# Spreads by transposes, fewer exponent instructions, a conv tap on ScalarE and bias rows spread in DRAM, in an SSM stage

## The reference

```
zxbcdt = rms_norm(x, ln_g) @ in_w          # 40 tiles of 128 columns, and dt
xbc = silu(causal_dwconv(xbc, conv_w, conv_b))        # 4 taps
a_cs = cumsum(a, axis=-1)                  # per head, chunks of 128 tokens
decay_in = exp(segsum(a))                  # exp(a_cs[l] - a_cs[s]), l >= s
y_diag = einsum('bclgn,bcsgn->bcgls', cc, bc) * decay_in @ xc
states = einsum(bc, exp(a_cs[..., -1:] - a_cs), xc)
y_off  = einsum(cc, states_in, exp(a_cs))
...
bias = rel_bias[t5_bucket(dist)]           # attention, 8 heads
```

## Time and profile before

| | |
|---|---|
| median of 3 runs | 2348.98 us (2348.26 to 2349.67) |
| profiled execution | 2351.74 us |
| its span | 2349.9 us |
| PE busy in the span | 2226.8 us, 95% |
| DVE busy | 1483.0 us, 63% |
| ACT busy | 914.2 us, 39% |
| granted TensorE clock, mean | 0.965 |

### The profile page before, as it was taken

The page is one execution under the profiler, slowest core; times in us unless marked ns, Lnnn a source line. Parts: engine busy times, 40 slices in busy tenths (PEclk is TensorE's granted clock), DMA queues, the critical chain, the costliest instruction groups (busy, mean ns, idle before and its releaser), DMA issues.

```text
span 2349.9 us, 26916 instructions
## 1 busy us (share of the span) xinstructions
PE 2226.8 (95%) x10370; PEld 1686.4 (72%) x10370; DVE 1483.0 (63%) x2262; ACT 914.2 (39%) x1379; POOL 0.2 (0%) x4
## 2 busy tenths in 40 slices
PE   8998989999999998999799999998999999899997
PEld 6787775548888886777588888886666667677545
DVE  6588887647777336777677776455566746455334
ACT  4344443114444223777434443233354422343302
POOL 0000000000000000000000000000000000000000
PEclk9998999999999998999799999998999999899999
DMA  4321111123232333111023222332122123111122
GB/s 143 108 65 53 55 63 45 45 81 94 94 98 87 94 101 103 54 55 55 21 96 98 95 94 88 93 110 72 54 70 68 60 72 135 37 46 48 43 83 79
DMA packets 53245, 179.39 MB, mean 76 GB/s; under 512 B 5751, under 2 KB 5879, under 8 KB 52888
## 3 DMA queue, kind: packets, MB, share of 16 engines
q1 hardware_dynamic: 50112, 167.79, 22.7%
q10 hardware_dynamic: 3032, 10.28, 1.2%
HBM read 173.33 MB, written 4.72 MB: 76 GB/s over the span
## 4 chain that ended last, share of the span: by engine, by line
PE 43%; DVE 7%; ACT 2%; issue 1%; DMA 0%; DVEq 0%; ACTq 0%
PE bankpair L271 11%; PE bankpair L272 11%; PE bankpair L275 11%; PE bankpair L279 4%; DVE conv_rows L352 1%; PE bankpair L1200 1%; PE bankpair L1233 1%; PE bankpair L1214 1%; DVE weights_low L306 1%; DVE reciprocals L1473 1%; PE bankpair L1066 1%; DVE padded_rows L1424 1%; ACT L1304 0%; PE bankpair L1075 0%; PE bankpair L1182 0%
## 5 line engine op out<-in xcount | busy, mean ns | idle before, releaser
L271 PE MATMUL bankpair<-scaled_in_high,weights_high 128*128 128x512 f32 x1792 | 731.0, 408 | 12.9 <-DVE padded_rows L1939 4.3
L272 PE MATMUL bankpair<-scaled_in_low,weights_high 128*128 128x512 f32 x1792 | 709.2, 396 | 0.0
L275 PE MATMUL bankpair<-scaled_in_high,weights_low 128*128 128x512 f32 x1792 | 447.9, 389 | 0.0
L295 ACT ACTIVATE weights_high<-weight_ring 128x1024 fp32r<-128x1024 f32 (+2 forms) x304 | 302.5, 995 | 348.1 <-DMA weight_ring<-down_dram 155.8
L271 PEld LDWEIGHTS bankpair<-scaled_in_high,weights_high 128*128 128x128 f32 x1792 | 344.1, 192 | 96.9 <-issue 13.1
L272 PEld LDWEIGHTS bankpair<-scaled_in_low,weights_high 128*128 128x128 f32 x1792 | 343.6, 192 | 76.0 <-issue 6.1
L275 PEld LDWEIGHTS bankpair<-scaled_in_high,weights_low 128*128 128x128 f32 x1792 | 336.7, 188 | 70.3
L306 DVE TENSOR_TENSOR weights_low<-weight_ring,weights_high 128x1024 fp32r<-128x1024 f32 (+2 forms) x304 | 347.8, 1154 | 55.2 <-ACT weights_high L295 46.7
L279 PE MATMUL bankpair<-arena,weight_ring 128*128 128x512 f32 x448 | 199.4, 607 | 2.8 <-DVE arena L1975 1.5
L279 PEld LDWEIGHTS bankpair<-arena,weight_ring 128*128 128x128 f32 x448 | 86.9, 195 | 111.2 <-issue 107.4
L271 PE MATMUL bankpair<-gated_high,weights_high 128*128 128x512 f32 x352 | 139.2, 396 | 0.0
(11 more groups left out here) (325 smaller groups left out, 2456.9 us busy)
## 6 DMA issues: line engine op xcount, KB each, us to landing
weight_ring<-up_dram SPq DMA_DIRECT2D x88, 512.0 KB, 3.4
weight_ring<-w_in_dram SPq DMA_DIRECT2D x70, 512.0 KB, 3.4
weight_ring<-in_w_dram SPq DMA_DIRECT2D x40, 512.0 KB, 3.5
weight_ring<-down_dram SPq DMA_DIRECT2D x32, 384.0 KB, 3.1
weight_ring<-kvq_dram SPq DMA_DIRECT2D x24, 512.0 KB, 3.4
weight_ring<-down_dram SPq DMA_DIRECT2D x32, 320.0 KB, 2.8
weight_ring<-out_a_dram SPq DMA_DIRECT2D x8, 512.0 KB, 3.4
weight_ring<-out_b_dram SPq DMA_DIRECT2D x8, 512.0 KB, 3.5
```

The costliest lines, as they stand in the source:

```text
L271: nc.tensor.matmul(bank, WH[:, high_slot, cell], high, start=(k == 0), stop=False)
L272: nc.tensor.matmul(bank, WH[:, high_slot, cell], low, start=False, stop=False)
L275: mm = nc.tensor.matmul(bank, WL[:, slot, cell], high, start=False, stop=(c == last_k))
L295: nc.scalar.activation(WH[:, (PART0[name] + k) % SLOTS, 0:n], RAW[:, b % SLOTS, 0:n], ACT.Copy).then_inc(high_ready, 1)
```

## The change

- The sums of a unit are spread by eight transposes of a repeated column of `CSTK` (tokens on partitions) in place of eight products.
- One minimum on 128x1024, min(spread sums, own sum), takes the place of the eight subtractions with a minimum; the own sum is subtracted by the bias of the exponential, so that ACT runs eight exponentials of 128x128. The last column of the result serves in place of `FX`, so that its copies, its difference and its exponential go. The two exponentials of the spread sums become one.
- DVE's order in a unit: the copy of the last exponentials and the product with C now stand before the wait for ACT, the scaling for the state and the product with C B behind it; the last releases PE's y.
- The first conv tap of the 24 x, B and C rows is an ACT instruction (Identity with scale and bias), ahead of ACT's weight split; DVE waits for it before the other three.
- The bias rows of all eight heads are one pair of products with eight columns behind tile 0, one copy (8x640), one write to DRAM; eight DRAM to DRAM transfers, one behind each of rows 2 to 9 on ACT's queue, spread them over 128 rows. Attention's read waits for them.

```diff
+        BROWS = nc.dram_tensor("bias_rows", (AH, 640), F32, kind="Internal").ap()
...
+        def first_tap(act, b, taps_and_bias, taps):
+            return nc.scalar.activation(CV[:, b, :], U[:, b, 3:3 + T], ACT.Identity, bias=taps_and_bias(taps),
+                                        scale=taps_and_bias(taps - 1))
+        def other_taps(step, done, b, taps_and_bias, taps):
+            for k in range(taps - 1):
+                at = 3 - (taps - 1) + k
+                (done if k == taps - 2 else step).step(nc.vector.scalar_tensor_tensor(
+                    CV[:, b, :], U[:, b, at:at + T], taps_and_bias(k), CV[:, b, :], ALU.mult, ALU.add))
...
+            act.wait_ge(brow_spread, 16 * AH)
             skewed = bass.AP(tensor=DSCR.tensor, offset=P - 1, ap=[[639, P], [P * 640, AH], [1, T]])
@@ PE
             for j in range(GROUP_TILES):
                 in_tile(0, j)
-                if j >= GROUP_TILES - AH:
-                    bias_row(j - (GROUP_TILES - AH))
+                if j == 0:
+                    pe.wait_ge(aux_in, 32)
+                    nc.tensor.matmul(BANK[2][0:AH, :], REL[0:33, :], BUCK[0:33, 0:T], start=True, stop=True)
+                    nc.tensor.matmul(BANK[3][0:AH, 0:P], REL[0:33, :], BUCK[0:33, T:640],
+                                     start=True, stop=True).then_inc(brow_done, 1)
...
                     for h in range(SSM_HG):
-                        nc.tensor.matmul(BANK[2 + h // 4][:, (h % 4) * P:(h % 4 + 1) * P],
-                                         IDENT[0:32, SSM_HG * g + h:SSM_HG * g + h + 1].to_broadcast([32, P]),
-                                         CSR[0:32, tok], start=True, stop=True)
+                        nc.tensor.transpose(BANK[2 + h // 4][:, (h % 4) * P:(h % 4 + 1) * P],
+                                            CSTK[:, c, SSM_HG * g + h:SSM_HG * g + h + 1].to_broadcast([P, P]), IDENT)
@@ ACT
             def rows(g, j):
                 n = GROUP_TILES * g + j
+                if j >= GT:
+                    act.wait_ge(gemm_free, TILE0["in_w"] + n + 1)
+                    first_tap(act, n % 2, ssm_taps(g, j), 4).then_inc(row_tap, 1)
                 split_high(act, BASE["in_w"] + n + 3)
...
                 rows(0, j)
-                b = j - (GROUP_TILES - AH)
-                if b >= 0:
-                    act.wait_ge(brow_done, b + 1)
-                    nc.scalar.activation(BROW[:, b, 0:T], BANK[2][:, :], ACT.Copy).then_inc(brow_ready, 1)
-                    nc.scalar.activation(BROW[:, b, T:640], BANK[3][:, 0:P], ACT.Copy).then_inc(brow_ready, 1)
-            act.wait_ge(brow_ready, 2 * AH)
-            act.dma_start(DSCR.rearrange("h p m -> p h m"), BROW).then_inc(brow_out, 16)
+                if j == 0:
+                    act.wait_ge(brow_done, 1)
+                    nc.scalar.activation(BROW[0:AH, :], BANKPAIR[1][0:AH, :, :].rearrange("p a t -> p (a t)")[:, 0:640],
+                                         ACT.Copy).then_inc(brow_ready, 1)
+                    act.wait_ge(brow_ready, 1)
+                    act.dma_start(BROWS, BROW[0:AH, :]).then_inc(brow_out, 16)
+                if j == 2:
+                    act.wait_ge(brow_out, 16)
+                if j >= GROUP_TILES - AH:
+                    b = j - (GROUP_TILES - AH)
+                    act.dma_start(DSCR[b], BROWS[b:b + 1, :].to_broadcast([P, 640])).then_inc(brow_spread, 16)
...
-                    for q in range(2):
-                        nc.scalar.activation(ECS[:, 4 * q:4 * q + 4, :],
-                                             BANK[2 + q][:, :].rearrange("p (h t) -> p h t", t=P),
-                                             ACT.Exp).then_inc(e_ready, 1)
+                    nc.scalar.activation(ECS, BANKPAIR[1][:, :, :].rearrange("p a (h t) -> p (a h) t", t=P),
+                                         ACT.Exp).then_inc(e_ready, 1)
                     act.wait_ge(d_ready, u + 1)
-                    nc.scalar.activation(DEC, DEC, ACT.Exp).then_inc(d_exp, 1)
-                    nc.scalar.activation(FX, FX, ACT.Exp).then_inc(d_exp, 1)
+                    for h in range(SSM_HG):
+                        at = SSM_HG * g + h
+                        exp = nc.scalar.activation(DEC[:, h, :], DEC[:, h, :], ACT.Exp, bias=NEGCS[:, c, at:at + 1])
+                    exp.then_inc(d_exp, 1)
@@ DVE
                 if j >= GT:
-                    conv(dve, step, cv, n % 2, lambda k: par("ssm_conv", 5 * ((GT + 2) * g + j - GT) + k), 4)
+                    dve.wait_ge(row_tap, (GT + 2) * g + j - GT + 1)
+                    other_taps(step, cv, n % 2, ssm_taps(g, j), 4)
...
             tt.step(nc.vector.tensor_copy(CSTK, b6[:, :, 32:64]))
+            tt.step(nc.vector.tensor_scalar(NEGCS, CSTK, -1.0, None, ALU.mult))
...
-                    for q in range(2):
-                        step.step(nc.vector.tensor_copy(etot[:, 4 * q:4 * q + 4], BANK[2 + q][:, P - 1:T:P]))
-                    step.step(nc.vector.tensor_tensor(fx, etot, CSTK[:, c, heads], ALU.subtract))
-                    for h in range(SSM_HG):
-                        ins = nc.vector.tensor_scalar(dec[:, h, :], BANK[2 + h // 4][:, (h % 4) * P:(h % 4 + 1) * P],
-                                                      CSTK[:, c, SSM_HG * g + h:SSM_HG * g + h + 1], 0.0,
-                                                      ALU.subtract, ALU.min)
-                    dr.step(ins)
-                    dve.wait_ge(d_exp, 2 * u + 2)
-                    step.step(nc.vector.tensor_tensor(dec, dec, CBM.unsqueeze(1).to_broadcast([P, SSM_HG, P]), ALU.mult))
+                    dr.step(nc.vector.tensor_tensor(dec, BANKPAIR[1][:, :, :].rearrange("p a (h t) -> p (a h) t", t=P),
+                                                    CSTK[:, c, heads].unsqueeze(2).to_broadcast([P, SSM_HG, P]), ALU.min))
                     step.step(nc.vector.tensor_copy(etot, ecs[:, :, P - 1]))
-                    mce.step(nc.vector.tensor_tensor(ecs, ecs, xb[:, GT + 1, tok].unsqueeze(1).to_broadcast([P, SSM_HG, P]),
-                                                     ALU.mult))
+                    step.step(nc.vector.tensor_tensor(ecs, ecs, xb[:, GT + 1, tok].unsqueeze(1).to_broadcast([P, SSM_HG, P]),
+                                                      ALU.mult))
+                    dve.wait_ge(d_exp, u + 1)
                     if c < NT - 1:
-                        xf.step(nc.vector.tensor_tensor(x_f, xdt, fx.unsqueeze(2).to_broadcast([P, SSM_HG, 64]), ALU.mult))
+                        xf.step(nc.vector.tensor_tensor(x_f, xdt, dec[:, :, P - 1:P].to_broadcast([P, SSM_HG, 64]), ALU.mult))
+                    mce.step(nc.vector.tensor_tensor(dec, dec, CBM.unsqueeze(1).to_broadcast([P, SSM_HG, P]), ALU.mult))
```

More of the change, by code:

```diff
@@ L175, in three_parts @@
         conv_ready = sem("tile_rows_ready")
+        row_tap = sem("ssm_first_taps_ready")
         exp_set = sem("exp_tables_asked_for")
@@ L199, in three_parts @@
         brow_out = sem("bias_rows_in_dram")
+        brow_spread = sem("bias_rows_spread_in_dram")
+        BROWS = nc.dram_tensor("bias_rows", (AH, 640), F32, kind="Internal").ap()
         DSCR = nc.dram_tensor("bias_scratch", (AH, P, 640), F32, kind="Internal").ap()
@@ L353, in conv, with ssm_taps @@
                     y, u[:, at:at + T], taps_and_bias(k), y, ALU.mult, ALU.add))
+        def first_tap(act, b, taps_and_bias, taps):
[6 more added lines that the diff above has]
+                    CV[:, b, :], U[:, b, at:at + T], taps_and_bias(k), CV[:, b, :], ALU.mult, ALU.add))
+        def ssm_taps(g, j):
+            return lambda k: par("ssm_conv", 5 * ((GT + 2) * g + j - GT) + k)
         mb = Carve()
@@ L365, in three_parts @@
         BTOK = mb(P)
-        FX = mb(SSM_HG)
         ETOT = mb(SSM_HG)
@@ L378, in three_parts @@
         CSTK = mb(NT, 32)
+        NEGCS = mb(NT, 32)
         UNITS = SSM_G * NT
@@ L382, in three_parts @@
         bb = Carve()
-        bb.at = 3 * T
-        BROW = bb(AH, 640)
+        bb.at = 3 * GT * T
+        BROW = bb(640)
         BUCK = bb(640)
@@ L1724, in _ @@
             pe.wait_ge(loaded, 16)
-            def bias_row(h):
-                if h >= 1:
-                    pe.wait_ge(brow_ready, 2 * h)
-                nc.tensor.matmul(BANK[2][:, :], REL[0:33, h:h + 1].to_broadcast([33, P]), BUCK[0:33, 0:T],
-                                 start=True, stop=True)
-                nc.tensor.matmul(BANK[3][:, 0:P], REL[0:33, h:h + 1].to_broadcast([33, P]), BUCK[0:33, T:640],
-                                 start=True, stop=True).then_inc(brow_done, 1)
             def in_tile(g, j):
                 gemm_tile(pe, "in_w", 0, GROUP_TILES * g + j, lambda k: (HH[:, k, :], HL[:, k, :]))
-            pe.wait_ge(aux_in, 32)
             for j in range(GROUP_TILES):
                 in_tile(0, j)
-                if j >= GROUP_TILES - AH:
-                    bias_row(j - (GROUP_TILES - AH))
+                if j == 0:
[3 more added lines that the diff above has]
```

(10 more changed lines are left out.)

3 lines of the change are left out of this document (2 added, 1 removed).

## The result

The changed kernel takes 2307.47 us (median of 4 runs, 2306.19 to 2312.88) against 2349.32 us before: 42 us less, ratio 0.9829, 95% interval 0.9817 to 0.9841. The forecast was 2315 us, 34 less, in a range of 2301 to 2329. The profiled execution took 2308.31 us; its span is 2306.5 us, 43.4 less than before.

The account below looks back on a forecast made before the run. PE was taken to bound the first tiles and last group, DVE's chain units 1 to 11. 10.4+8.3+16.6+2.9-4 = 34 us off the profiled 2351.7 gives 2317.5, with the median 2.8 lower: 2315 us, range 2301 to 2329.

Parts of the forecast that it names:

- the three regimes: SSM stage: PE sets the pace up to the first unit, DVE's chain in units 1 to 11, PE in 12 to 15.
- The first tiles: First group of tiles: bias pairs, first tap and ACT copies off the path, together 10.4 us less.
- The exponentials: ACT's eight per unit: started 0.30 us apart, 2.64 us in all, leaving DVE a wait of 1.18 us.
- A DVE unit: DVE's work in one unit: 4.04 us replaced by a 1.27 us minimum and a 1.18 us wait, 1.59 us less.
- The tap: First conv tap moved from DVE to ACT: hidden there, 0.58 us a row, 3.5 us a group.
- Groups 1 and 2: Second and third groups, paced by DVE: three shorter units and the taps, 8.3 us less each.
- the clock term: Three group starts: tiles move nearer the wait, so more half-speed time hits them; 4 us charged, between gain 3 and loss 9.
- unit 0: First unit, after PE's 4.44 us wait: shorter spreads and transposes, gain of 1.0 to 1.9 us, taken as 1.4.
- the last stretch: Last group, paced by PE: 2.9 us less, 1.0 in three units and 0.9 in the first.
- The slower rival: PE falls to half clock at every unit, as 13 transposes stand in one piece: 2354 to 2369 us; chance 0.04.
- falls at inner units: Sign of being wrong: granted clock of 0.5 at inner units; clock falls were expected at group starts only.
- Behind the stage: Everything after the SSM stage: only moved, so zero us of change.

Follow-up runs that it names:

- u_tap: The changed kernel with the first conv tap back on DVE; 2320.18 us, ratio 0.9873.
- u_spread: The changed kernel with the spreads as products of 32 rows again; 2317.85 us, ratio 0.9862.
- x_full: The changed kernel with the spreads as products of 128 rows in place of transposes; 2310.31 us, ratio 0.9830.
- b_spread: The kernel before with only the spreads changed, to transposes; 2340.20 us, ratio 0.9961.
- v_fill2: The kernel of v_fill run once more; 2307.19 us, ratio 0.9821.
- v_fill: The changed kernel with DVE's product of x with the skip weights moved ahead of the wait for the exponentials; 2306.88 us, ratio 0.9819.

## Why the prediction was right or wrong

**Right.** What bounds the kernel: the three regimes held. The first tiles: 10.4 forecast and measured, 9.5 by undoing them. The exponentials: I chose the pace of 0.30 us from the row with a bias column, and the wait came out at 1.13 against 1.18. A DVE unit lost 1.7 us against 1.59. The Trainium skill, *ScalarE: Activation LUTs*, "What ACT_TABLE_LOAD costs", gives an estimated 387 ns for one by its formula; the trace shows 387 (L1907, median). The tap: 0.58 us a row, and 10.6 in all against 11, where the total is in part luck (`u_tap`). Groups 1 and 2, which rest on these, gave 9.2 and 8.6 against 8.3 each.

**Wrong in size: the clock term and unit 0.** The step "Now the spreads are short and end before the last silu ..., so the tiles start nearer to the wait. A whole slow stretch costs half of some 9 us" took the 9 us of the earlier trace rows as a fixed length after a restart, and so charged 4 us. The length wasn't fixed, and neither was the fall. 5.1 of these 9 us were the 32-row spreads and the transposes behind them, and in unit 0 `u_spread` and `x_full` show that with the 32-row spreads the clock stays at half longer. With them gone it came back there by 88. At the starts of the third and the last group it didn't fall at all; only at unit 4 does it still, from 164 to 170. In all the clock misses 6.5 us of the stage instead of 22.2.

The transposes alone don't explain the two starts without a fall. `b_spread` and `u_tap` have transposes and fall at unit 8; PE stands there for 3.7 us in one piece, ahead of the spreads. In the changed kernel the wait is in two pieces, 1.79 us ahead of the spreads and 2.47 behind them. But that isn't enough either: `v_fill2` waits for 0.84 and the same 2.47 us there and falls. Its stretches at unit 8:

```profile
248.00:250.00 2.00, 2.00 (x7) 1.54 (x6) 1.03 (x3) 1.96 (x5) 0.00 (x0) 0.60 0.00 0
250.00:252.00 2.00, 2.00 (x6) 1.55 (x5) 1.38 (x2) 0.71 (x1) 0.00 (x0) 0.54 0.03 8
```

and those of the changed kernel:

```profile
250.00:252.00 2.00, 0.45 (x4) 0.46 (x5) 1.90 (x4) 1.12 (x2) 0.00 (x0) 1.00 0.00 0
252.00:254.00 2.00, 2.00 (x10) 1.63 (x10) 1.66 (x4) 1.91 (x5) 0.00 (x0) 1.00 0.00 0
```

And at unit 12 the one kernel of `v_fill` and `v_fill2` has both. So the missing falls at units 8 and 12, which both profiles of the changed kernel have in common, can't be put down to the transposes alone; how much of them is luck, and what decides it, stays open. The stretches at the start of the last group, before:

```profile
376.00:378.00 2.00, 1.66 (x5) 1.15 (x6) 1.90 (x4) 1.88 (x4) 0.00 (x0) 0.50 0.00 0
```

and after:

```profile
336.00:338.00 2.00, 1.51 (x6) 0.96 (x7) 1.90 (x4) 1.92 (x3) 0.00 (x0) 1.00 0.00 0
```

I put this down as the 3.6 us by which the last stretch beat its forecast (6.5 against 2.9), and with unit 0 (105.57 against 119.57, so 14.0-10.4 = 3.6 against 1.4) most of the rest: the stage ended some 12 us better than forecast (46.3 against 34), of which 4 are the charge for the clock, 3.3 the way to unit 4, 1.2 groups 1 and 2, and 3.6 the last group. The transposes were priced at 4.3 less 4 for the clock; undoing them costs 11.0, of which 6.0 are shown to be theirs.

**The slower rival** had the sign of that effect wrong. At inner units there are two falls, at 202 and at 288, and both stand at a wait of 3.38 us before y, ahead of the transposes; the kernel before has such a fall too, at 226. The prediction had named falls at inner units as a sign of being wrong and expected them at group starts only; that line of it was wrong. No piece of 13 transposes let the clock fall. The Trainium skill, *TensorE: Matmul & The Clock Gate*, "Part 4: PE-mode transpose", has transposes not count as PE-busy the same way; in unit 0 the clock was back 2.8 us after the restart with transposes and 3.2 with products of 128 rows, so there the measurement speaks against the rule.

**Behind the stage** I had put zero. 2.9 us were given back, some 2.6 of them at one place, where the second block's small products wait for a load. Busy time by stretch, before:

```profile
1990.00:1994.00 4.00, 1.94 (x36) 1.67 (x32) 0.00 (x0) 0.64 (x1) 0.00 (x0) 1.00 0.96 410
1994.00:1998.00 4.00, 2.67 (x50) 2.68 (x52) 0.00 (x0) 0.00 (x0) 0.00 (x0) 1.00 0.02 8
1998.00:2002.00 4.00, 4.00 (x78) 4.00 (x74) 0.00 (x0) 0.00 (x0) 0.00 (x0) 1.00 0.02 4
```

and after:

```profile
1944.00:1948.00 4.00, 1.56 (x30) 1.29 (x24) 0.00 (x0) 0.30 (x1) 0.00 (x0) 1.00 0.90 375
1948.00:1952.00 4.00, 2.16 (x28) 1.98 (x30) 0.00 (x0) 0.00 (x0) 0.00 (x0) 0.82 0.03 12
1952.00:1956.00 4.00, 4.00 (x58) 3.76 (x56) 0.00 (x0) 0.00 (x0) 0.00 (x0) 0.75 0.00 0
```

PE waits 3.4 us for that load before and 4.3 after, and after it the granted clock is 0.82 and 0.75 in two stretches where it stayed at 1.00 before. Over all my profiles the time from the last y to the end of the span lies between 1893.0 (`b_spread`) and 1900.0 (`u_tap`) for unchanged work; the changed kernel had 1897.5 twice. So up to 7 us of a comparison of totals here may not be the change's. What decides whether the clock falls there stays open. That 42 and not 34 us were saved is more than this: at the end of the stage, ahead of it, it was 46.3.

## What to carry to other kernels

Before pricing a wait or a half-speed stretch as a constant, read what PE does while it lasts: here going back to eight products of 32 rows a unit cost 11 us, of which only 2.7 were the second pass, at least 3.3 a longer slow stretch of the clock, and the rest falls that may or may not be theirs. One profile of a kernel doesn't show whether a fall belongs to it: the kernel of `v_fill` has none at the last group's start in one profile and one in the other. An instruction with a column operand is priced from a row that has one; 0.13 us each made the difference between a wait of 1.1 and of 0.1. And when the rest of a long program varies by itself, compare a mark at the end of the changed stage, not the total.

## What the runs showed of the hardware that I had not expected

- In unit 0, after a wait of 3.9 to 5.0 us, TensorE's granted clock stood at 0.50. With spreads of 128 rows, transposes or products, it was back at 1.00 2.8 to 5.0 us after the restart (twelve profiles); with spreads of 32 rows after 9.0 (`u_spread`) and 8.0 us (the kernel before). The operand that is the identity was exchanged with the number of rows, so the two aren't told apart.
- The same wait of 2.47 us ahead of the same instruction, at unit 8, came with a fall of the clock in `v_fill2` (0.60 and 0.54) and without one in the changed kernel (1.00).
- Eight spreads of 320 KB from DRAM to DRAM landed in 4.2 us each beside the weight stream, whose pieces took 3.9 us instead of 3.5; between 30 and 84 us no engine waited for a DMA.
